# Keys of the latent attention formed channels first, with the weight columns stationary, in a two-block fp32 kernel on one core

## The chip, the core and the metric

The kernel runs on one core of one Trainium2 chip. The metric is the device time of one execution, in microseconds (us); the median of three executions of the kernel before is 2329.42 us (2329.14 to 2329.72). The core has TensorE (matrix products, PE in the profile, with PEld for its weight loads), VectorE (DVE), ScalarE (ACT), GpSimd (POOL) and SyncE (SP), which issues the DMAs. A matmul has a stationary operand, which a weight load puts into the array, and a moving operand, of which one column after another streams past it.

## The reference, cut to what matters

256 tokens of width 2048 go through a first block (pooling mixer, gated linear attention, a feed-forward part) and then through two layers of a second block. Only the second block's layers are touched by the change, and of them only the keys and values:

```python
for l in range(2):
    z = rmsnorm(x, pre_norm_g[l]) @ w_in[l]
    q_lat, kv_lat, k_pe, gb, gc, xin, q_mem, gate = split_cols(z)
    q = (rmsnorm(q_lat, q_norm_g[l]) @ w_uq[l]).reshape(b, s, 8, 192)
    kv = (rmsnorm(kv_lat, kv_norm_g[l]) @ w_ukv[l]).reshape(b, s, 8, 128 + 128)
    k_nope, v = kv[..., :128], kv[..., 128:]
    k = concatenate([k_nope, broadcast(apply_rope(k_pe, cos, sin))], axis=-1)
    a_out = mla_attention(q, k, v)      # softmax(q k^T / sqrt(192)) v, 8 heads
    ...
    x = x + rmsnorm(concatenate([a_out, c_out, m_out]) * silu(gate) @ w_o[l], post_norm_g[l])
```

`kv_lat` has 256 channels and `w_ukv` is 256 x 2048: for each of the 8 heads 128 columns of keys and 128 of values. The scores need the keys with the channels on the partitions; the product with the probabilities needs the values with the tokens on the partitions.

## The kernel before, in words

All products are made in fp32 precision from two fp32r parts each: a value is split into a high part and the rest (low), and a product is the sum of three matmuls, high by high, high by low and low by high. The weights are streamed from HBM once. `weight_groups` (from L92) lists them in the order of use as groups, mostly of 512 columns by 16 slices of 128 rows. A group's slices are its **steps**: `Plan` (from L180) numbers them through the whole kernel, and two steps of a group share a slab, one load into a buffer `raw`. ScalarE copies a slab to its high part `wh` (L1493), VectorE subtracts to get the low part `wl` (L2123), and TensorE uses both.

TensorE's main loop (in `tensor_program`, from L612) makes for each step the products for both halves of the 256 tokens: the activation slice (128 channels by 128 tokens) is stationary, the 512 weight columns move, and the output has the tokens on the partitions (L998 to L1000). That is six matmuls a step. The sums of a group lie in `pm`, two pairs of PSUM banks used in turn, so a group's sums must be taken out by the time the next group but one begins.

All else is **background work**, written by hand as generators with the step at which each piece is due: `layer(l)` exists once in each of `tensor_program`, `scalar_program` and `vector_program`. Each `yield L + n` means "when step n of this layer is reached", L being the first step of the group `ql`. TensorE does a piece in between its steps. ScalarE and VectorE do theirs ahead of the split of the slab that lies three slabs in front of that step (`Plan.ahead`, L208), and each engine's queue is strictly in order, so that a wait in a piece holds up the slabs behind it.

The steps of a layer are: ql 0 to 15 (query latents), kv 16 to 31 (key latents and rotary key), qm 32 to 47, a gate group 48 to 63, uq0 64 to 67, a gate group, uq1 84 to 87, **ukv0 88 and 89**, a gate group, uq2, **ukv1 110 and 111**, a gate group, uq3, **ukv2 132 and 133**, gc, **ukv3 150 and 151**, xi, gb, then the output product. `uq` j and `ukv` j hold the queries and the keys and values of two heads. `ROUNDS` (L245) has the steps of the six attention rounds: scores, turn of the probabilities, product with the values, turn of the output; rounds 2 to 5 use ukv0 to ukv3, and their scores are due at steps 96, 118, 140 and 158.

What happens to the keys before, for each of the four `ukv` groups of each of the two layers:

- The latents (group kv) are taken out of PSUM by ScalarE, scaled by the root of the earlier norm, their squares are summed (L1038), and VectorE (L1532) and GpSimd (`inverse_root`, L577) make the latents' own root from it, `rs["kv"]`. Meanwhile TensorE turns the unscaled latents at step 35 (`lat_turns`), ScalarE and VectorE make the high and low part of the turned latents with the norm's gain (`high_gain` and `low_gain`), `kvT`. At step 38 the rotary key is turned (`kp_t`).
- The main loop makes two steps of six matmuls of 512 columns with `kvT` stationary.
- `ukv_taken` (L1112): ScalarE takes the result, tokens first, in four instructions, scaling each token's row by `rs["kv"]`: keys to `S2` (L1126), values to `vt` (L1128).
- `uk_turn` (L861), at steps 93, 115, 137 and 155 (`UK`): TensorE turns the keys of two heads, four transposes of 128 by 128 (all transposes have the line of the helper `turn`, L628), into bank 7.
- `uk_copy` (L1131): ScalarE copies bank 7 to the high part of `kT` (L1136), VectorE subtracts for the low part (L1513, in `low`).
- The scores (L814 to L818) use `kT` as moving operand of 256 columns.

Of the kernel before, what the change touches and what calls it, by code (L numbers as in the profile page):

```python
# [14 lines left out]
T = 256  # L15
# [76 lines left out]
def weight_groups(a):  # L92
# [3 lines left out]
    def add(name, act, w, c0, n=512, kts=k16, **more):  # L96
        out.append(Group(name, act, [(w[:, c0:c0 + n], n)], kts, **more))
# [41 lines left out]
    for l in range(2):  # L139
# [7 lines left out]
        def ukv(j):  # L147
            add(f"ukv{l}{j}", "kvT", w_kv, 512 * j, kts=range(2), ev=("a", 4))

# [69 lines left out]
def counted(parts):  # L219

    out, n = {}, 0
    for name, w in parts:
# [23 lines left out]
          (158, 162, 165, 169))  # L246
UQ_N, UQ_R, UK = (71, 91, 113, 135), (79, 95, 117, 139), (93, 115, 137, 155)
S2_OF = {"ql": 0, "kv": 1, "qm": 0, "uq0": 1, "uq1": 0, "ukv0": 1, "uq2": 0, "ukv1": 1, "uq3": 0, "ukv2": 1, "gc": 0,
         "ukv3": 1}
SEMAPHORES = """mm hi lo ev_a ev_d nh sq st_r st_v rstd scl sq0 warm xsq xrd xss msq mrd mss hT_h hT_l pool_m wp_h wp_l dT_h dT paT_h paT_l gu g_h la_m la_d la_a qk_t  # L250
qk_c sc_m g_c sd sc_e e_m lev_m dg v_h at_d a_h av_m on_d oT_t oT_h oT_l sig mix_d mix_t mix_h mix_l mem_h mem_l rp rp_a xr xt_t
xt_h xt_l mk_t mk_c f_t f_h f_l fs_d sc mx ex rl pt_t pt_c pv ys yt_t y_h y_l ql_t ql_h ql_l kv_t kv_h kv_l kp_t kp_c qm_t
qm_c qm_l mk_h mk_l kp_l uq_t uq_c uq_l uqr_t uqr_c uqr_l uk_t uk_c uk_l u_t u_c cv_d gb_t gbm c_h c_l half d_id d_t0 d_t1 d_t2 d_t3 d_t4 d_t5 d_t6 d_gain d_pm d_wp d_wgu d_bg
d_cm d_bi0 d_bi1 d_bc d_pos d_m0 d_m1 d_m2 d_m3 d_x d_out""".split() + [f"raw{i}" for i in range(NRAW)]
# [357 lines left out]
def tensor_program(nc, s, m, p):  # L612
# [6 lines left out]
    def free(b):  # L619
        if b in bank:  # L620
            w.wait_ge(s[bank[b][0]], bank[b][1])
# [153 lines left out]
    def lat_turns(l, name, n, at0):  # L775

        S = m.S2[S2_OF[name]]
        for i in range(n):
            yield at0 + i
            free(6 + i)  # L780
            w.wait_ge(s["ev_a"], p.evac[f"{name}{l}"])
            turn_pair(6 + i, S, 2 * i).then_inc(s[f"{name}_t"], 1)
            bank[6 + i] = (f"{name}_l", (l * n + i + 1) * 2)

    def attention(l, r, which):

        idx = 2 * (6 * l + r)
        if which == 0:
# [15 lines left out]
            else:  # L804
                w.wait_ge(s["uq_l"], 4 * l + r - 1)
                w.wait_ge(s["uqr_l"], 2 * (4 * l + r - 1))
                w.wait_ge(s["uk_l"], 4 * l + r - 1)
                w.wait_ge(s["kp_l"], l + 1)
                w.wait_ge(s["ev_a"], p.evac[f"ukv{l}{r - 2}"])
                (qh_, ql_), (kh_, kl_) = m.qT[j], m.kT[j]  # L810
# [49 lines left out]

    def uk_turn(l, j):  # L861
        free(7)
        w.wait_ge(s["ev_a"], p.evac[f"ukv{l}{j}"])
        turn_pair(7, m.S2[S2_OF[f"ukv{j}"]], 0).then_inc(s["uk_t"], 1)
        bank[7] = ("uk_l", 4 * l + j + 1)

    def layer(l):
        L = p.first[f"ql{l}"]
        yield from lat_turns(l, "ql", 2, L + 19)
        yield from lat_turns(l, "kv", 1, L + 35)  # L870
        yield L + 38
        free(7)
# [20 lines left out]
        uq_turn(l, 1)  # L893
        yield L + UK[0]
        uk_turn(l, 0)
        yield L + UQ_R[1]
        uqr_turn(l, 1)
        for r in range(2, 6):
            for which in range(4):
                yield L + ROUNDS[r][which]  # L900
                attention(l, r, which)
            if r < 4:
                yield L + UQ_N[r]
                uq_turn(l, r)
            if r < 5:
                yield L + UK[r - 1]
                uk_turn(l, r - 1)
            if r < 4:
                yield L + UQ_R[r]
                uqr_turn(l, r)  # L910
# [40 lines left out]
    for i, g in enumerate(p.groups):  # L951
# [4 lines left out]
        for k in g.kts:  # L956
# [31 lines left out]
            elif n == 0:  # L988
                for x, y, sem in ((ah, h, "hi"), (al, h, "hT_l"), (ah, l, "lo")):
                    w.wait_ge(s[sem], 1)  # L990
                    for half in range(2):
                        ins = e.matmul(acc[:, half, :], x[:, 0, half * 128:half * 128 + 128], y[:, c], start=(sem == "hi"),
                                       stop=False)
            else:
                for half in range(1 if g.name == LAST else 2):
# [23 lines left out]
def scalar_program(nc, s, m, xT, lead, p):  # L1019
# [92 lines left out]
    def ukv_taken(l, j):  # L1112
        name = f"ukv{l}{j}"
        acc = m.pm[p.groups.index(p.g[name]) % 2]
        S = m.S2[S2_OF[f"ukv{j}"]]
        w.wait_ge(s["rstd"], RS[f"kv{l}"])
        w.wait_ge(s["mm"], p.end[name])
        if j == 0:
            w.wait_ge(s["sc"], 12 * l + 4)
            w.wait_ge(s["uq_t"], 4 * l + 1)  # L1120
            w.wait_ge(s["rp"], RP[f"uq{l}0"])
        else:
            w.wait_ge(s["uk_t"], 4 * l + j)
        for half in range(2):
            av = acc[:, half, :].rearrange("p (h d) -> p h d", h=2)
            e.activation(S[:, half, 0:256].rearrange("p (h d) -> p h d", h=2), av[:, :, 0:128], ACT.Copy,  # L1126
                         scale=m.rs[f"kv{l}"][:, half:half + 1]).then_inc(s["ev_a"], 1)
            e.activation(m.vt[:, half, 2 * j:2 * j + 2, :], av[:, :, 128:256], ACT.Copy,  # L1128
                         scale=m.rs[f"kv{l}"][:, half:half + 1]).then_inc(s["ev_a"], 1)

    def uk_copy(l, j):  # L1131
        w.wait_ge(s["uk_t"], 4 * l + j + 1)
        w.wait_ge(s["pv"], 12 * l + 4)
        if j >= 2:
            w.wait_ge(s["sc"], 12 * l + 2 * j + 2)
        e.activation(m.kT[j % 2][0][:, :, :], view(7), ACT.Copy).then_inc(s["uk_c"], 1)  # L1136

# [30 lines left out]
    def layer(l):  # L1168
# [19 lines left out]
        if l:  # L1188
            w.wait_ge(s["u_t"], 2)
            w.wait_ge(s["uk_t"], 4)  # L1190
        taken(0, f"ql{l}", m.S2[0], scale=f"r{r}")
# [9 lines left out]
        for half in range(2):  # L1201
            w.wait_ge(s["ev_a"], p.evac[f"kv{l}"])
            squares(m.S2[1][:, half, 0:256], m.ssq[f"kv{l}"][:, half:half + 1])
        yield L + 36
        w.wait_ge(s["kv_t"], l + 1)
        high_gain(6, m.kvT[0], 0, f"kv{l}", 0, "kv_h")
        w.wait_ge(s["mk_c"], 2 * l + 2)
        e.activation(m.mkS[0][:, :, :], m.mkT[l][:, :, :], ACT.Copy).then_inc(s["mk_h"], 1)
        yield L + 39
        w.wait_ge(s["kp_t"], l + 1)  # L1210
# [33 lines left out]
        uq_copy(l, 1)  # L1244
        yield L + UK[0] + 1
        uk_copy(l, 0)
        yield L + UQ_R[1] + 1
        uqr_copy(l, 1)
        for rr in range(2, 6):
# [18 lines left out]
            if rr < 4:  # L1268
                yield L + UQ_N[rr] + 1
                uq_copy(l, rr)  # L1270
            if rr < 5:
                yield L + UK[rr - 1] + 1
                uk_copy(l, rr - 1)
            if rr < 4:
# [227 lines left out]
def vector_program(nc, s, m, p):  # L1502
# [113 lines left out]
    def memory_low(n, c):  # L1616
        yield p.first[MEM_FROM[n]] + MEM_SPLITS[n][c] + 1
        piece = (m.memA, m.memB)[n][c // 2]
        if n:
            w.wait_ge(s["u_t"], 2)  # L1620
            w.wait_ge(s["uk_t"], 4)
            w.wait_ge(s["c_h"], 2)
            w.wait_ge(s["c_l"], 2)
# [113 lines left out]
    def layer(l):  # L1737
# [11 lines left out]
        if l:  # L1749
# [3 lines left out]
        e.tensor_copy(m.kpd[:, :, 64:128], m.kpd[:, :, 0:64]).then_inc(s["rp"], 1)  # L1753
        yield L + 36
        low_gain(6, m.kvT, 0, f"kv{l}", 0, "kv_h", 2 * l + 2, "kv_l")
        w.wait_ge(s["mk_h"], l + 1)
        e.tensor_tensor(m.mkS[1][:, :, :], m.mkT[l][:, :, :], m.mkS[0][:, :, :].bitcast(F32), ALU.subtract
                        ).then_inc(s["mk_l"], 1)
        yield L + 39
        low(7, m.kpeT, 0, 1, "kp_c", l + 1, "kp_l")  # L1760
# [3 lines left out]
        for r in range(6):  # L1764
# [33 lines left out]
            if 1 <= r <= 4:  # L1798
                yield L + UK[r - 1] + 1
                low(7, m.kT[(r - 1) % 2], 0, 2, "uk_c", 4 * l + r, "uk_l")  # L1800
            if 1 <= r <= 3:
# [394 lines left out]
```

## Time and profile before

| | us |
|---|---|
| median of three executions | 2329.42 (2329.14 to 2329.72) |
| the profiled execution's own time | 2329.7 |
| its span, first to last instruction | 2327.9 |
| around the span | 1.8 |
| TensorE busy | 2318.0 |
| TensorE weight loads busy | 1940.5 |
| VectorE busy | 1359.2 |
| ScalarE busy | 1180.9 |
| DMA engines' mean busy share | 62% |
| granted TensorE clock, mean | 0.999 of full |

A row of the timeline has the start of an instruction (or of a run of like ones, with their count) in us from the span's start, its duration in us, the engine, the line, what it writes and reads, the size of the stationary operand, and the partitions by columns of the moving one. Matmuls overlap: the end of one is modelled and lies behind the start of the next, so what a matmul costs in a dense stream is the distance from its start to the next one's start, not its duration.

### The profile page before, as it was taken

Reading aid. Unit: us, or ns where it says so; the run is one execution under the profiler, and the core shown is the slowest. Engines: PE = TensorE matmul, PEld = TensorE weight load, DVE = VectorE, ACT = ScalarE, POOL = GpSimd, SP = SyncE. Lnnn points to the kernel's source line nnn. Section 1 sums busy time; section 2 is a strip of 40 time slices with the busy share of each in tenths; the row PEclk is TensorE's granted clock in tenths of the full one; section 3 lists DMA queues with packets and bytes.
Section 4 is the critical chain, followed back from the end, with each engine's and each line's share of the span. In section 5 each row is a group of like instructions: output and inputs, shape, how many; then the busy total and the mean of one; then the engine's idle time right before and its main releaser. Section 6 shows DMA issues by size and latency. Waiting matters only on the chain.

```text
span 2327.9 us, 27235 instructions
## 1 busy us (share of the span) xinstructions
PE 2318.0 (100%) x10941; PEld 1940.5 (83%) x10941; DVE 1359.2 (58%) x1721; ACT 1180.9 (51%) x1565; POOL 25.6 (1%) x35
## 2 busy tenths in 40 slices
PE   9999999999999999999999999999999999999998
PEld 7888888888888888888888888888888888888887
DVE  6677666555566644554445555575555656565564
ACT  6555655444445744444444344465555456565543
POOL 0000000000000000000000000000000000000000
PEclk9999999999999999999999999999999999999999
DMA  8666665666667566665666666666555665655564
GB/s 292 189 176 172 173 171 176 195 200 199 191 206 268 173 192 190 190 189 190 192 190 192 191 190 206 223 179 191 158 159 163 199 217 154 196 162 150 157 204 136
DMA packets 237837, 438.87 MB, mean 189 GB/s; under 512 B 16688, under 2 KB 42800, under 8 KB 237072
## 3 DMA queue, kind: packets, MB, share of 16 engines
q1 hardware_dynamic: 237280, 436.61, 61.9%
q8 instruction: 86, 1.41, 0.2%
q10 hardware_dynamic: 432, 0.53, 0.1%
q14 instruction: 39, 0.32, 0.0%
HBM read 434.99 MB, written 2.10 MB: 188 GB/s over the span
## 4 chain that ended last, share of the span: by engine, by line
PE 99%; DMA 0%; DVE 0%; ACT 0%; SPq 0%; DVEq 0%; issue 0%; ACTq 0%
PE pm L998 31%; PE pm L1000 31%; PE pm L999 31%; PE pb L628 3%; PE pb L835 1%; PE pb L721 1%; PE pb L731 0%; DMA raw<-in_w_in 0%; PE pb L817 0%; PE pb L815 0%; PE pb L816 0%; PE pb L818 0%; PE pb L814 0%; PE pm L1015 0%; PE pm L1014 0%; PE pm L1016 0%
## 5 line engine op out<-in xcount | busy, mean ns | idle before, releaser
L2123 DVE TENSOR_TENSOR wl<-raw,wh 128x1024 fp32r<-128x1024 f32 (+3 forms) x786 | 949.2, 1211 | 846.2 <-ACT wh L1493 844.2
L1493 ACT ACTIVATE wh<-raw 128x1024 fp32r<-128x1024 f32 (+3 forms) x786 | 820.4, 1046 | 934.7 <-PE pm L1000 930.4
L998 PE MATMUL pm<-wh,hTh 128*128 128x512 f32 x702 | 277.4, 395 | 1.4 <-DVE wl L2123 1.3
L998 PE MATMUL pm<-wh,x2Th 128*128 128x512 f32 x704 | 275.3, 391 | 0.0
L1000 PE MATMUL pm<-wh,x2Tl 128*128 128x512 f32 x704 | 274.1, 389 | 0.0
L999 PE MATMUL pm<-wl,x2Th 128*128 128x512 f32 x704 | 274.0, 389 | 0.0
L1000 PE MATMUL pm<-wh,hTl 128*128 128x512 f32 x702 | 273.7, 390 | 0.0
L999 PE MATMUL pm<-wl,hTh 128*128 128x512 f32 x702 | 273.4, 389 | 0.0
L998 PE MATMUL pm<-wh,xT3h 128*128 128x512 f32 (+1 forms) x640 | 251.6, 393 | 0.0
L1000 PE MATMUL pm<-wh,xT3l 128*128 128x512 f32 (+1 forms) x640 | 245.0, 383 | 0.0
L999 PE MATMUL pm<-wl,xT3h 128*128 128x512 f32 (+1 forms) x640 | 244.5, 382 | 0.0
L998 PEld LDWEIGHTS pm<-wh,hTh 128*128 128x128 f32 x702 | 131.9, 188 | 29.2 <-DVE wl L2123 3.3
L1000 PEld LDWEIGHTS pm<-wh,x2Tl 128*128 128x128 f32 x704 | 132.2, 188 | 27.6
L1000 PEld LDWEIGHTS pm<-wh,hTl 128*128 128x128 f32 x702 | 131.8, 188 | 28.0
L999 PEld LDWEIGHTS pm<-wl,x2Th 128*128 128x128 f32 x704 | 132.2, 188 | 27.0
L998 PEld LDWEIGHTS pm<-wh,x2Th 128*128 128x128 f32 x704 | 132.2, 188 | 26.9
L999 PEld LDWEIGHTS pm<-wl,hTh 128*128 128x128 f32 x702 | 132.0, 188 | 25.8
L1000 PEld LDWEIGHTS pm<-wh,xT3l 128*128 128x128 f32 x640 | 120.1, 188 | 23.5
L999 PEld LDWEIGHTS pm<-wl,xT3h 128*128 128x128 f32 x640 | 120.6, 188 | 19.9
L998 PEld LDWEIGHTS pm<-wh,xT3h 128*128 128x128 f32 x640 | 120.4, 188 | 19.7
L998 PE MATMUL pm<-wh,yTh 128*128 128x512 f32 x240 | 93.7, 391 | 0.0
L1000 PE MATMUL pm<-wh,yTl 128*128 128x512 f32 x240 | 93.4, 389 | 0.0
(414 smaller groups left out, 3125.0 us busy)
## 6 DMA issues: line engine op xcount, KB each, us to landing
raw<-in_w_in SPq DMA_DIRECT2D x286, 512.0 KB, 3.7
raw<-in_w_ffn_gate SPq DMA_DIRECT2D x88, 512.0 KB, 4.3
raw<-in_w_ffn_up SPq DMA_DIRECT2D x88, 512.0 KB, 3.8
raw<-in_w_ffn_down SPq DMA_DIRECT2D x88, 512.0 KB, 4.1
raw<-in_w_o SPq DMA_DIRECT2D x64, 512.0 KB, 4.4
raw<-in_w_in SPq DMA_DIRECT2D x68, 256.0 KB, 3.2
raw<-in_w_branch_b SPq DMA_DIRECT2D x32, 512.0 KB, 3.7
raw<-in_w_out SPq DMA_DIRECT2D x32, 512.0 KB, 4.5
```

Source lines behind the costliest of these rows:

```text
L628: ins = e.transpose(pb[b][:, o:o + 128], src[half], ident[:, :])
L721: ins = e.matmul(pb[4 + i][:, j * 128:j * 128 + 128], E[:, 4 * i + j, 0, ft, :], E[:, 4 * i + j, 1, ft, :], start=(ft == 0), stop=(ft == 1))
L835: ins = e.matmul(pb[4 + ln][:, qh * 128:qh * 128 + 128], m.PT[ln][:, kk, qh * 128:qh * 128 + 128], v, start=(kk == 0), stop=(kk == 1))
L998: e.matmul(o, ah[:, kk, t], h[:, c], start=first, stop=False)
L999: e.matmul(o, ah[:, kk, t], l[:, c], start=False, stop=False)
L1000: ins = e.matmul(o, al[:, kk, t], h[:, c], start=False, stop=last)
L1493: e.activation(h[:, 0:n], r[:, 0:n], ACT.Copy).then_inc(s["hi"], 1)
L2123: e.tensor_tensor(l[:, 0:n], r[:, 0:n], h[:, 0:n].bitcast(F32), ALU.subtract).then_inc(s["lo"], 1)
```

## The change

The keys of the two heads of a `ukv` group are formed channels first, so that they need no turn. The columns of `w_ukv` are put in another order in HBM: in each group of 512 the keys of both heads come first, the values of both heads behind them. For the key columns the weight slice (128 rows by 128 columns) is now the stationary operand and the 256 tokens of `kvT` move; for the value columns the activation stays stationary and 256 weight columns move. A token's scale can no longer be applied per partition to keys whose tokens lie along the free dimension, so the latents themselves are scaled by `rs["kv"]` before they are turned. `uk_turn`, `uk_copy` and the staging of the keys in `S2` are gone; the latents' turn and what follows from it is due four steps later, the rotary key's three.

```diff
         def ukv(j):
-            add(f"ukv{l}{j}", "kvT", w_kv, 512 * j, kts=range(2), ev=("a", 4))
+            add(f"ukv{l}{j}", "kvT", w_kv, 512 * j, kts=range(2), ev=("d", 1))
...
-UQ_N, UQ_R, UK = (71, 91, 113, 135), (79, 95, 117, 139), (93, 115, 137, 155)
+UQ_N, UQ_R = (71, 91, 113, 135), (79, 95, 117, 139)
...   tensor_program, lat_turns
             w.wait_ge(s["ev_a"], p.evac[f"{name}{l}"])
+            if name == "kv":
+                w.wait_ge(s["kv_s"], 2 * l + 2)
...   tensor_program, attention (scores)
-                w.wait_ge(s["uk_l"], 4 * l + r - 1)
                 w.wait_ge(s["kp_l"], l + 1)
-                w.wait_ge(s["ev_a"], p.evac[f"ukv{l}{r - 2}"])
+                w.wait_ge(s["ev_d"], p.evac[f"ukv{l}{r - 2}"])
...
-    def uk_turn(l, j):
-        free(7)
-        w.wait_ge(s["ev_a"], p.evac[f"ukv{l}{j}"])
-        turn_pair(7, m.S2[S2_OF[f"ukv{j}"]], 0).then_inc(s["uk_t"], 1)
-        bank[7] = ("uk_l", 4 * l + j + 1)
...   tensor_program, layer (and its four calls of uk_turn are gone)
-        yield from lat_turns(l, "kv", 1, L + 35)
-        yield L + 38
+        yield from lat_turns(l, "kv", 1, L + 39)
+        yield L + 41
...   tensor_program, main loop
+            elif g.name.startswith("ukv"):
+
+                for b in range(2):
+                    o, c = acc[:, 0, b * T:(b + 1) * T], slice(at0 + b * 128, at0 + b * 128 + 128)
+                    e.matmul(o, h[:, c], ah[:, kk, :], start=first and b == 0, stop=False, skip_group_check=True)
+                    e.matmul(o, l[:, c], ah[:, kk, :], start=False, stop=False, skip_group_check=True)
+                    e.matmul(o, h[:, c], al[:, kk, :], start=False, stop=last, skip_group_check=True)
+                c = slice(at0 + 256, at0 + 512)
+                for half in range(2):
+                    o, t = acc[:, 1, half * T:(half + 1) * T], slice(half * 128, half * 128 + 128)
+                    e.matmul(o, ah[:, kk, t], h[:, c], start=first and half == 0, stop=False, skip_group_check=True)
+                    e.matmul(o, ah[:, kk, t], l[:, c], start=False, stop=False, skip_group_check=True)
+                    ins = e.matmul(o, al[:, kk, t], h[:, c], start=False, stop=last, skip_group_check=True)
...   scalar_program, ukv_taken
-        S = m.S2[S2_OF[f"ukv{j}"]]
-        w.wait_ge(s["rstd"], RS[f"kv{l}"])
         w.wait_ge(s["mm"], p.end[name])
-        if j == 0:
-            w.wait_ge(s["sc"], 12 * l + 4)
-            w.wait_ge(s["uq_t"], 4 * l + 1)
-            w.wait_ge(s["rp"], RP[f"uq{l}0"])
-        else:
-            w.wait_ge(s["uk_t"], 4 * l + j)
-        for half in range(2):
-            av = acc[:, half, :].rearrange("p (h d) -> p h d", h=2)
-            e.activation(S[:, half, 0:256].rearrange("p (h d) -> p h d", h=2), av[:, :, 0:128], ACT.Copy,
-                         scale=m.rs[f"kv{l}"][:, half:half + 1]).then_inc(s["ev_a"], 1)
-            e.activation(m.vt[:, half, 2 * j:2 * j + 2, :], av[:, :, 128:256], ACT.Copy,
-                         scale=m.rs[f"kv{l}"][:, half:half + 1]).then_inc(s["ev_a"], 1)
-
-    def uk_copy(l, j):
-        w.wait_ge(s["uk_t"], 4 * l + j + 1)
+        w.wait_ge(s["sc"], 12 * l + 4)
         w.wait_ge(s["pv"], 12 * l + 4)
         if j >= 2:
             w.wait_ge(s["sc"], 12 * l + 2 * j + 2)
-        e.activation(m.kT[j % 2][0][:, :, :], view(7), ACT.Copy).then_inc(s["uk_c"], 1)
+        e.activation(m.vt[:, :, 2 * j:2 * j + 2, :], acc[:, 1, :].rearrange("p (a h d) -> p a h d", a=2, h=2), ACT.Copy
+                     ).then_inc(s["uk_c"], 1)
+        e.activation(m.kT[j % 2][0][:, :, :], acc[:, 0, :].rearrange("p (n t) -> p n t", n=2), ACT.Copy
+                     ).then_inc(s["uk_c"], 1)
...   scalar_program, layer (and its calls of uk_copy are gone)
-        yield L + 36
+        yield L + 37
+        w.wait_ge(s["rstd"], RS[f"kv{l}"])
+        for half in range(2):
+            e.activation(m.S2[1][:, half, 0:256], m.S2[1][:, half, 0:256], ACT.Copy, scale=m.rs[f"kv{l}"][:, half:half + 1]
+                         ).then_inc(s["kv_s"], 1)
+        yield L + 40
         w.wait_ge(s["kv_t"], l + 1)
         high_gain(6, m.kvT[0], 0, f"kv{l}", 0, "kv_h")
         w.wait_ge(s["mk_c"], 2 * l + 2)
         e.activation(m.mkS[0][:, :, :], m.mkT[l][:, :, :], ACT.Copy).then_inc(s["mk_h"], 1)
-        yield L + 39
+        yield L + 42
         w.wait_ge(s["kp_t"], l + 1)
...   vector_program, layer (the latents' low part is due at L + 40 in place of 36, the rotary key's at 42 in place of 39)
             if 1 <= r <= 4:
-                yield L + UK[r - 1] + 1
-                low(7, m.kT[(r - 1) % 2], 0, 2, "uk_c", 4 * l + r, "uk_l")
+                yield p.end[f"ukv{l}{r - 1}"] + 1
+                w.wait_ge(s["uk_c"], 2 * (4 * l + r))
+                k, acc = m.kT[(r - 1) % 2], banks(f"ukv{l}{r - 1}")
+                e.tensor_tensor(k[1][:, :, :], acc[:, 0, :].rearrange("p (n t) -> p n t", n=2), k[0][:, :, :].bitcast(F32),
+                                ALU.subtract).then_inc(s["ev_d"], 1)
...   kernel (host side, order of the weight's columns)
+    arrays["w_ukv_2"] = np.ascontiguousarray(
+        arrays["w_ukv_2"].reshape(2, 256, 4, 2, 2, 128).transpose(0, 1, 2, 4, 3, 5)).reshape(2, 256, 2048)
```

Three waits on the removed semaphore `uk_t`, which guard the reuse of `S2` and of the memory pieces, become waits on `uq_t`.

## Rows read from the trace of the kernel before

**Rows 1.** The page: busy times, granted clock by slice, and the chain that ended last.

```profile
PE 2318.0 (100%) x10941; PEld 1940.5 (83%) x10941; DVE 1359.2 (58%) x1721; ACT 1180.9 (51%) x1565; POOL 25.6 (1%) x35
...
PEclk9999999999999999999999999999999999999999
...
PE 99%; DMA 0%; DVE 0%; ACT 0%; SPq 0%; DVEq 0%; issue 0%; ACTq 0%
```

**Rows 2.** All waits of TensorE in the whole span: us in total, times, longest.

```profile
PE pb L947 <- POOL warm L570: 1.3, 1, 1.3
PE pm L998 <- DVE wl L2123: 1.3, 2, 0.7
```

**Rows 3.** Timeline of TensorE, group ukv0 of the first layer, first and last of 12.

```profile
1684.48 0.39 PE L998 MATMUL pm<-wh,kvTh 128*128 128x512 f32 x1
...
1687.01 0.39 PE L1000 MATMUL pm<-wh,kvTl 128*128 128x512 f32 x1
1687.24 0.39 PE L998 MATMUL pm<-wh,xT3h 128*128 128x512 f32 x1
```

**Rows 4.** Timeline of TensorE, a turn of keys and the 18 matmuls behind it.

```profile
1793.63 0.60 PE L628 MATMUL pb<-ident,s 128*128 128x128 f32 x4
1793.98 0.48 PE L998 MATMUL pm<-wh,xT3h 128*128 128x512 f32 x1
1794.29 0.40 PE L999 MATMUL pm<-wl,xT3h 128*128 128x512 f32 x1
...
1797.97 0.39 PE L1000 MATMUL pm<-wh,xT3l 128*128 128x512 f32 x1
1798.19 0.28 PE L814 MATMUL pb<-kT1h,qT1h 128*128 128x256 f32 x1
```

**Rows 5.** Timeline of TensorE, 18 matmuls of 512 columns, nothing between; first and last.

```profile
1700.39 0.39 PE L998 MATMUL pm<-wh,xT3h 128*128 128x512 f32 x1
...
1704.25 0.39 PE L1000 MATMUL pm<-wh,xT3l 128*128 128x512 f32 x1
```

**Rows 6.** Timeline of TensorE, 20 score matmuls: the first, and the matmul behind them.

```profile
1696.61 0.28 PE L814 MATMUL pb<-kT0h,qT0h 128*128 128x256 f32 x1
...
1699.01 0.40 PE L998 MATMUL pm<-wh,xT3h 128*128 128x512 f32 x1
```

**Rows 7.** The same for the 48 matmuls of the low-rank gate group, weights stationary.

```profile
57.11 0.28 PE L985 MATMUL pm<-hTh,wh 128*96 128x256 f32 x1
...
62.76 0.40 PE L998 MATMUL pm<-wh,hTh 128*128 128x512 f32 x1
```

**Rows 8.** Weight loads of one score line: ns min/median/max, first and last start.

```profile
L815 PEld LDWEIGHTS pb<-kT0l,qT0h x16: 188/188/192, 1696.6 to 2161.9; 128*128 128x128 f32 x16
```

**Rows 9.** The keys' and values' way through ScalarE and VectorE, by tile, same columns.

```profile
L1126 ACT ACTIVATE s<-pm,st x16: 473/475/476, 1687.5 to 2182.9; 128x256 f32<-128x256 f32 x16
L1128 ACT ACTIVATE vt<-pm,st x16: 467/475/482, 1687.9 to 2183.3; 128x256 f32<-128x256 f32 x16
L1136 ACT ACTIVATE kT0h<-pb x4: 598/598/600, 1692.4 to 2155.9; 128x512 fp32r<-128x512 f32 x4
L1513 DVE TENSOR_TENSOR kT0l<-pb,kT0h x4: 691/692/692, 1693.1 to 2156.5; 128x512 fp32r<-128x512 f32 x4
```

**Rows 10.** Timelines of ScalarE, GpSimd, VectorE and TensorE around the latents' turn.

```profile
1600.76 0.42 ACT L1038 ACTIVATE junk<-s 128x256 f32<-128x256 f32 x1
...
1601.17 2.00 ACT L1493 ACTIVATE wh<-raw 128x1024 fp32r<-128x1024 f32 x2
1603.78 0.84 ACT L1047 ACTIVATE kvTh<-pb,gain 128x256 fp32r<-128x256 f32 x2 [0.61 <-PE pb L628]
...
1601.55 0.77 POOL L577 TENSOR_TENSOR st<-st 128x2 f32<-128x2 f32 x1 [13.43 <-DVE st L1532]
...
1606.74 1.22 DVE L2123 TENSOR_TENSOR wl<-raw,wh 128x1024 fp32r<-128x1024 f32 x1
...
1613.39 0.39 PE L998 MATMUL pm<-wh,xT3h 128*128 128x512 f32 x1
```

More of the change, by code:

```diff
@@ L246 @@
           (158, 162, 165, 169))
-UQ_N, UQ_R, UK = (71, 91, 113, 135), (79, 95, 117, 139), (93, 115, 137, 155)
-S2_OF = {"ql": 0, "kv": 1, "qm": 0, "uq0": 1, "uq1": 0, "ukv0": 1, "uq2": 0, "ukv1": 1, "uq3": 0, "ukv2": 1, "gc": 0,
-         "ukv3": 1}
+UQ_N, UQ_R = (71, 91, 113, 135), (79, 95, 117, 139)
+S2_OF = {"ql": 0, "kv": 1, "qm": 0, "uq0": 1, "uq1": 0, "uq2": 0, "uq3": 0, "gc": 0}
 SEMAPHORES = """mm hi lo ev_a ev_d nh sq st_r st_v rstd scl sq0 warm xsq xrd xss msq mrd mss hT_h hT_l pool_m wp_h wp_l dT_h dT paT_h paT_l gu g_h la_m la_d la_a qk_t
@@ L252 @@
 xt_h xt_l mk_t mk_c f_t f_h f_l fs_d sc mx ex rl pt_t pt_c pv ys yt_t y_h y_l ql_t ql_h ql_l kv_t kv_h kv_l kp_t kp_c qm_t
-qm_c qm_l mk_h mk_l kp_l uq_t uq_c uq_l uqr_t uqr_c uqr_l uk_t uk_c uk_l u_t u_c cv_d gb_t gbm c_h c_l half d_id d_t0 d_t1 d_t2 d_t3 d_t4 d_t5 d_t6 d_gain d_pm d_wp d_wgu d_bg
+qm_c qm_l mk_h mk_l kp_l uq_t uq_c uq_l uqr_t uqr_c uqr_l kv_s uk_c u_t u_c cv_d gb_t gbm c_h c_l half d_id d_t0 d_t1 d_t2 d_t3 d_t4 d_t5 d_t6 d_gain d_pm d_wp d_wgu d_bg
 d_cm d_bi0 d_bi1 d_bc d_pos d_m0 d_m1 d_m2 d_m3 d_x d_out""".split() + [f"raw{i}" for i in range(NRAW)]
@@ L893, in layer @@
         uq_turn(l, 1)
-        yield L + UK[0]
-        uk_turn(l, 0)
         yield L + UQ_R[1]
@@ L904, in layer @@
                 uq_turn(l, r)
-            if r < 5:
-                yield L + UK[r - 1]
-                uk_turn(l, r - 1)
             if r < 4:
@@ L1189, in layer @@
             w.wait_ge(s["u_t"], 2)
-            w.wait_ge(s["uk_t"], 4)
+            w.wait_ge(s["uq_t"], 4)
         taken(0, f"ql{l}", m.S2[0], scale=f"r{r}")
@@ L1244, in layer @@
         uq_copy(l, 1)
-        yield L + UK[0] + 1
-        uk_copy(l, 0)
         yield L + UQ_R[1] + 1
@@ L1270, in layer @@
                 uq_copy(l, rr)
-            if rr < 5:
-                yield L + UK[rr - 1] + 1
-                uk_copy(l, rr - 1)
             if rr < 4:
@@ L1620, in memory_low @@
             w.wait_ge(s["u_t"], 2)
-            w.wait_ge(s["uk_t"], 4)
+            w.wait_ge(s["uq_t"], 4)
             w.wait_ge(s["c_h"], 2)
@@ L1753, in layer @@
         e.tensor_copy(m.kpd[:, :, 64:128], m.kpd[:, :, 0:64]).then_inc(s["rp"], 1)
-        yield L + 36
+        yield L + 40
         low_gain(6, m.kvT, 0, f"kv{l}", 0, "kv_h", 2 * l + 2, "kv_l")
@@ L1758, in layer @@
                         ).then_inc(s["mk_l"], 1)
-        yield L + 39
+        yield L + 42
         low(7, m.kpeT, 0, 1, "kp_c", l + 1, "kp_l")
```

## The prediction

> **What bounds the kernel.** I read the page first. TensorE is busy for 2318.0 of 2327.9 us, the chain that ended last is 99% TensorE, and the granted clock stands at its full level in all slices [rows 1]. Busy time of matmuls can hide gaps, since their ends are modelled, so the second view is that of the waits: TensorE waits twice, 1.3 us each, both in the lead-in or the first block, and never in the two layers that the change touches [rows 2]. So the time of these layers is the sum of the distances between the starts of TensorE's instructions. What ScalarE, VectorE or GpSimd gain or lose costs nothing until it makes TensorE wait. The third view, the timeline of TensorE, gives the prices of the instructions that are swapped.
>
> **Prices on TensorE.** All are start-to-start distances.
> - A matmul of 512 columns in an undisturbed stream: 1704.25 - 1700.39 = 3.86 us for 17 distances, 0.227 us each [rows 5].
> - A `ukv` group before, 12 matmuls of 512 columns: 1687.24 - 1684.48 = 2.76 us, 0.230 each [rows 3].
> - A turn of keys, four transposes: from its start to the first score matmul are 1798.19 - 1793.63 = 4.56 us, and the 18 matmuls of 512 columns in between would take 18 x 0.2271 = 4.09 without it [rows 4, 5]. So a turn costs 0.47 us: 0.35 to the next matmul's start, 0.31 - 0.23 = 0.08 more on that one, and a remainder in the next few.
> - A matmul of 256 columns with 128 stationary columns: (1699.01 - 1696.61) / 20 = 0.120 us [rows 6]. With weights stationary (96 columns) and the activations moving, the very form that the keys take: (62.76 - 57.11) / 48 = 0.118 us [rows 7].
>
> **The sum, part by part.** There are 4 groups in each of 2 layers, 8 in all.
> 1. Removed: 8 turns of keys, 8 x 0.47 = 3.8 us. Nothing covers them, since they stand in TensorE's own stream. Their steps (93, 115, 137, 155) lie two steps or more from any other turn, so each one has its own tail to lose.
> 2. Changed: each group's 12 matmuls of 512 columns become 24 of 256. The columns that stream are the same, but the part of a matmul that doesn't scale with columns is paid twice as often. 24 x 0.120 = 2.88 us in place of 2.76, so +0.12; I add 0.02 for the first long matmul behind short ones (the one behind the scores starts within a dense run as well, so this is an estimate from the 0.23 against 0.227 of rows 3 and 5). +0.14 a group, 8 x 0.14 = +1.1 us. I take 0.120 and not 0.118, as the stationary operand is 128 columns wide again. The bounds: 24 x 0.118 = 2.83 (+0.07 a group, +0.6 in all) below, and above, half of a matmul of this group and the whole fixed part worked out below on top, 0.230 / 2 + 0.013 = 0.128 [rows 3], should the switch between two kinds of stationary operand or two PSUM banks cost something: 3.07, +0.31 a group, +2.5 in all.
> 3. Moved: the turn of the latents from step 35 to 39 and that of the rotary key from 38 to 41. The same instructions at another place in the same dense stream: 0. They still have slack, for `kvT` is first read at step 88 and the rotary key at 96. The copies of `mkS` move with them and are first read at step 56. No DMA moves; the reordered weight has the same loads.
> 4. Added on ScalarE: two scalings of the latents, about 0.42 us each by the squares of the same size [rows 10], and a wait for the latents' root. In ScalarE's queue the piece due at step 37 stands before the same slab as the piece at 36 did, where the kernel before waited for the turn until 1603.78 and idled 0.61 us. The root leaves GpSimd at 1601.55 + 0.77 = 1602.32, before ScalarE has even finished the two splits that start at 1601.17 and end at 1603.17 [rows 10]. So the new wait is met about 0.8 us before it is asked. Behind it in the queue stands the split of the slab for steps 42 and 43; its low part was finished at 1606.74 + 1.22 = 1607.96 and TensorE first uses it at 1613.39, a lead of 5.4 us [rows 10]. The scalings take the place of the copy that has moved away. Cost 0; if the cover were gone, only what exceeds 5.4 us would reach TensorE.
> 5. Removed from ScalarE: four takings of 0.475 us per group become one of 512 elements, about 0.60 by the copy of the same size; the copy to `kT` and VectorE's subtraction stay at 0.60 and 0.69 [rows 9], but read the group's own sums. ScalarE gains about 1.3 us a group, 10 us in all, and it isn't the bound: 0. The keys are ready earlier: before, they left for a turn at 93, with copy and subtraction behind it; now both follow the group's end at 90. The last group's (152) stand against scores due at 158, six steps of 1.36 us.
> 6. The sums' banks are now freed by VectorE's subtraction (`ev_d`), one step behind the group. The next user is the next group but one, 16 steps or more later: 0.
>
> Sum: -3.8 + 1.1 = -2.7 us. The profiled execution took 2329.7 us (span 2327.9 and 1.8 around it) and goes to 2327.0; against the median of 2329.42, which lies 0.3 below it, that is 2326.7.
>
> **A rule against the trace.** Rows 5 and 6 show a fixed part: 0.227 us for 512 columns and 0.120 for 256 leave 0.227 - 2 x (0.227 - 0.120) = 0.013 us per matmul that doesn't scale with the columns. The Trainium skill, "TensorE: Matmul & The Clock Gate", section "Back-to-back issue gap", has N/2.4 + 2.5 ns for a warm matmul, so a fixed part five times smaller. By that page, halving the columns and doubling the count would cost 12 x 2.5 ns = 0.03 us a group and 0.24 in all, and the sum would be about -3.5; the trace contradicts the figure, and the sum above goes by the trace.
>
> **Rivals.**
> - *The whole gain shows, or more* (faster by over 0.2%, that is over 4.7 us; about what a measurement of this kernel can tell from no change). Turns at 3.8, the lower bound of part 2 (+0.6), and a loss of the 0.003 us by which the matmuls near the keys' turns and in the groups are slower than undisturbed ones [rows 3, 5] for some 20 matmuls around each of 8 groups (0.5): -3.7. It takes a further 1 us from something the rows don't show. 2325.7 as worked out, 2324.5 if over the bound. Chance of passing 0.2%: 0.06.
> - *The freed time comes back as waits*, so that nothing is gained: TensorE reaches its steps sooner and finds a slab not yet split. For it: VectorE and ScalarE are busy over half of the span [rows 1]. Against it: no wait in these layers now, and a lead of 5.4 us at a crowded place [rows 2, 10], against 0.5 us gained at a time. 2329.4. Chance 0.05.
> - *The short matmuls are bound by their weight loads* (slower). A load takes 0.188 us [rows 8], longer than the 0.120 between two short matmuls. Were the loads not overlapped where the stationary operand comes from `wh` and `wl`, which ScalarE and VectorE are writing to at the same time in other slots, a group would take 24 x 0.188 = 4.51 us, 1.75 more than before, 8 x 1.75 = +14.0, less 3.8 for the turns: +10.2, 2339.6. It turns into a loss from (2.76 + 0.47) / 24 = 0.135 us per matmul on, and into one of over 0.2% from (2.76 + 0.47 + 4.7 / 8) / 24 = 0.159. Against it: the scores have the same loads and hold 0.120 for 20 in a row, and the gate group has the weights stationary at 0.118 [rows 6, 7]. Chance 0.04.
> - *The turns aren't really saved*, since the change only moves work: excluded by the diff; four transposes a group are gone and none is added.
>
> **How the numbers follow.** The forecast, -2.7 us, is 0.12% and lies within 0.2%; its chance, with its bounds, is 0.85. Its own range: best, -3.8 + 0.6 less 0.5 for the slower neighbours = -3.7; worst, with 0.128 per short matmul and turns at 0.43 (0.35 + 0.08 without the remainder), -3.4 + 2.5 = -0.9. From 2329.42 that is 2325.7 to 2328.5; the runs scatter by 0.3 either way. To hold the time 8 times in 10 I take 2325.3 to 2328.7, which leaves out the slow rival, the case without any gain and the part of the fast one beyond its terms. Faster by over 0.2%: 0.06. Slower by over 0.2%: 0.04. Within 0.2%: 0.90.
>
> **What the new profile would show.** Right: 32 transposes fewer (10941 matmuls become 10941 - 32 + 96 = 11005, apart from records missing); a `ukv` group of 24 rows that takes 2.85 to 2.95 us from its first start to the next group's; no wait of TensorE in the two layers; undisturbed matmuls at 0.227 still; ScalarE busy about 10 us less. Part 4 is wrong if ScalarE idles before the scaling for the root, or TensorE waits for `wl` or `kvT` around steps 37 to 45. Part 2 is wrong if the short matmuls stand more than 0.128 apart, and then the loads' start times say whether the load is late. The forecast as a whole fails if TensorE waits anywhere for more than a microsecond in the layers, or if the clock falls below its full level.

## The result and the profile after

The changed kernel takes 2326.31 us (median of 22 executions, 2326.05 to 2326.66) against 2329.80 us (22 executions, 2329.14 to 2330.28) of the kernel before on the same chips: 3.5 us less, a ratio of 0.9985 (95% interval 0.9979 to 0.9992). The forecast was 2326.7, no change beyond 0.2%, and the measured change is 0.15%. It was worked out as 2.7 us less than 2329.42; the 22 executions put the kernel before 0.4 us above that base, so the forecast time is closer (0.4 us) than the forecast difference (0.8 us). The profiled execution took 2326.3 us with a span of 2324.5 us.

The page of the changed kernel, the lines that answer to [rows 1], and all waits of TensorE, which answer to [rows 2]:

```profile
PE 2314.6 (100%) x11005; PEld 1943.7 (84%) x11005; DVE 1358.8 (58%) x1721; ACT 1174.0 (51%) x1545; POOL 25.5 (1%) x35
...
PEclk9999999999999999999999999999999999999999
...
PE 99%; DMA 0%; DVE 0%; ACT 0%; SPq 0%; issue 0%; DVEq 0%; ACTq 0%
```

```profile
PE pm L1000 <- DVE wl L2115: 1.4, 3, 0.8
PE pb L936 <- POOL warm L569: 1.3, 1, 1.3
```

The 11005 matmuls are the 10941 - 32 + 96 of the prediction. TensorE is still the whole chain, at the full clock, and its few waits lie ahead of the two layers: cut to the layers, the list of waits is empty for this kernel and for every experiment below, though the last experiment has a short wait that this list doesn't show. ScalarE is 6.9 us less busy.

The timeline of TensorE around ukv0 of the first layer, which answers to [rows 3]: the 24 matmuls of 256 columns, the 6 long ones behind them, the turn of a pair of queries, and the place where the turn of the keys stood.

```profile
1684.08 0.28 PE L987 MATMUL pm<-kvTh,wh 128*128 128x256 f32 x1
1684.20 0.28 PE L988 MATMUL pm<-kvTh,wl 128*128 128x256 f32 x1
1684.32 0.28 PE L989 MATMUL pm<-kvTl,wh 128*128 128x256 f32 x1
...
1684.79 0.28 PE L993 MATMUL pm<-wh,kvTh 128*128 128x256 f32 x1
...
1686.95 0.40 PE L1000 MATMUL pm<-wh,xT3h 128*128 128x512 f32 x1
...
1688.34 0.60 PE L627 MATMUL pb<-ident,s 128*128 128x128 f32 x4
1688.69 0.48 PE L1000 MATMUL pm<-wh,xT3h 128*128 128x512 f32 x1
...
1694.26 0.38 PE L627 MATMUL pb<-ident,rope_o 128*128 128x128 f32 x2
...
1695.86 0.28 PE L814 MATMUL pb<-kT0h,qT0h 128*128 128x256 f32 x1
```

The group takes 1686.95 - 1684.08 = 2.87 us, 0.120 per matmul, whether the weights (L987 to L989) or the activations (L993 to L995) are stationary. Before it took 2.76 [rows 3]. The six long matmuls behind it take 1688.34 - 1686.95 = 1.39, where the kernel before has 1.36:

```profile
1687.24 0.39 PE L998 MATMUL pm<-wh,xT3h 128*128 128x512 f32 x1
...
1688.60 0.60 PE L628 MATMUL pb<-ident,s 128*128 128x128 f32 x4
1688.96 0.48 PE L998 MATMUL pm<-wh,xT3h 128*128 128x512 f32 x1
...
1691.80 0.60 PE L628 MATMUL pb<-ident,s 128*128 128x128 f32 x4
1692.15 0.48 PE L998 MATMUL pm<-wh,xT3h 128*128 128x512 f32 x1
...
1695.01 0.38 PE L628 MATMUL pb<-ident,rope_o 128*128 128x128 f32 x2
```

These are the rows of the kernel before at the same place; the second transpose row is the keys' turn. From the first long matmul behind the queries' turn to the rotary part's turn there are 24 long matmuls in both: 1695.01 - 1688.96 = 6.05 us before, 1694.26 - 1688.69 = 5.57 after. One turn of keys cost 0.48 us there.

ScalarE and GpSimd around the latents' scaling, which answer to [rows 10]:

```profile
1600.36 0.42 ACT L1040 ACTIVATE junk<-s 128x256 f32<-128x256 f32 x1
...
1600.78 1.99 ACT L1482 ACTIVATE wh<-raw 128x1024 fp32r<-128x1024 f32 x2
1604.36 1.06 ACT L1482 ACTIVATE wh<-raw 128x1024 fp32r<-128x1024 f32 x1 [1.60 <-PE pm L1002]
1605.33 0.89 ACT L1196 ACTIVATE s<-s,st 128x256 f32<-128x256 f32 x2
...
1608.82 0.84 ACT L1049 ACTIVATE kvTh<-pb,gain 128x256 fp32r<-128x256 f32 x2 [0.68 <-PE pb L627]
```

```profile
1601.15 0.77 POOL L576 TENSOR_TENSOR st<-st 128x2 f32<-128x2 f32 x1 [13.44 <-DVE st L1521]
```

The root is there at 1601.92 and the scaling begins at 1605.33, right behind a split and with no idle time before it. The wait is met 3.4 us early.

The values and keys are now taken by one instruction each, which answer to [rows 9]:

```profile
L1122 ACT ACTIVATE vt<-pm x8: 598/598/599, 1687.1 to 2179.4; 128x512 f32<-128x512 f32 x8
...
L1124 ACT ACTIVATE kT0h<-pm x4: 591/591/591, 1687.6 to 2148.9; 128x512 fp32r<-128x512 f32 x4
L1791 DVE TENSOR_TENSOR kT0l<-pm,kT0h x4: 679/680/682, 1691.0 to 2152.2; 128x512 fp32r<-128x512 f32 x4
```

### The profile page after: what moved, and what is told of

It is laid out like the page before. It is cut to its first block, busy times and chain, and to the rows that moved or that the text cites. A ratio compares the mean times of both kernels' runs of the same rounds, so it can differ in the third digit from the quotient of the medians.

```text
span 2324.5 us, 27335 instructions
## 1 busy us (share of the span) xinstructions
PE 2314.6 (100%) x11005; PEld 1943.7 (84%) x11005; DVE 1358.8 (58%) x1721; ACT 1174.0 (51%) x1545; POOL 25.5 (1%) x35
## 4 chain that ended last, share of the span: by engine, by line
PE 99%; DMA 0%; DVE 0%; ACT 0%; SPq 0%; issue 0%; DVEq 0%; ACTq 0%
PE pm L1000 30%; PE pm L1002 30%; PE pm L1001 30%; PE pb L627 3%; PE pb L835 1%; PE pb L720 1%; PE pb L730 0%; DMA raw<-in_w_in 0%; PE pb L817 0%; PE pb L815 0%; PE pm L989 0%; PE pm L994 0%; PE pm L995 0%; PE pm L993 0%; PE pb L816 0%; PE pm L988 0%
```

## A ruler for half a microsecond

Medians of this kernel scatter by a few tenths, as much as some of the effects. The traces give a finer ruler. The first turn of the query latents in the first layer of the second block (step 19, the first row below) and the last matmul of the program (the second row) are the same instructions in all versions, and all instructions that the change touches lie between them. The kernel before, in its first profiled execution:

```profile
1586.72 0.60 PE L628 MATMUL pb<-ident,s 128*128 128x128 f32 x4
...
2320.37 0.39 PE L1016 MATMUL pm<-wh,yTl 128*128 128x512 f32 x1
```

and the changed kernel:

```profile
1586.32 0.60 PE L627 MATMUL pb<-ident,s 128*128 128x128 f32 x4
...
2317.02 0.39 PE L1018 MATMUL pm<-wh,yTl 128*128 128x512 f32 x1
```

The stretch is 733.65 us before and 730.70 after: **2.95 us** are gained in it, and 0.40 us of the traces' difference already stand at its start, where the edit changes nothing. Each experiment below is read on this ruler too; the two profiles of each of these two kernels agree on it to 0.01 us.

## The experiments

**The two kernels once more.**

> The kernel before once more, as a yardstick for the lead-in and the first block, in which the changed kernel's trace is 0.40 us ahead although the edit touches nothing there. Theory A (that part of the trace differs from execution to execution): this trace's first block, against the other trace of the same kernel, is off by some tenths too, either way. Rival (the 0.40 belongs to the build, since another program is laid out otherwise): this trace agrees with the other of the same kernel within 0.1 us up to step ql of the first layer. Time 2329.4 to 2330.0 us by both.

> The changed kernel once more, as a yardstick for its own trace and for the next runs. Theory A: 2326.3 us within 0.3; the distance to the kernel before inside the two layers is 2.9 to 3.0 us as in the first pair of traces, and what lies ahead of them differs by some tenths from the other trace of the same kernel. Rival (the 0.40 us in the first block belongs to the build): the first block is again 0.4 us ahead of the kernel before.

Measured: 2329.85 us (11 executions) for the kernel before, 2326.35 us (11) for the changed one. The new profile of the kernel before:

```profile
1586.47 0.60 PE L628 MATMUL pb<-ident,s 128*128 128x128 f32 x4
...
2320.12 0.39 PE L1016 MATMUL pm<-wh,yTl 128*128 128x512 f32 x1
```

The stretch is again 733.65; that of the changed kernel's second profile is 2317.21 - 1586.51 = 730.70 again. What lies ahead of it moves by 0.25 us between two profiles of the kernel before (1586.72 and 1586.47) and by 0.19 between two of the changed one (1586.32 and 1586.51), so most of the 0.40 us of the first pair is scatter of the lead-in, as theory A had it. Not all of it lies in the first microseconds: from the first long matmul behind the low-rank gate group [rows 7] (62.76 and 62.62 us in the two profiles of the kernel before, 62.58 and 62.75 in those of the changed one) to the stretch's start are 1523.96 and 1523.85 us before, 1523.74 and 1523.76 after. Two profiles of one kernel differ by 0.11 us there, the two kernels by 0.1 to 0.2, and the builds of the experiments below have 1523.75 to 1524.09 at the same place. So builds and executions both move this part, by tenths of a microsecond, where no edit touches it.

**Only the latents' scaling and the moves.** The kernel before with part 3 and 4 of the prediction alone; the keys are still made tokens first and turned. The four takings of each `ukv` group no longer scale the tokens, and VectorE's low parts move with the turns (not in the cut of the edit).

```diff
-        yield from lat_turns(l, "kv", 1, L + 35)
-        yield L + 38
+        yield from lat_turns(l, "kv", 1, L + 39)      # waits for kv_s
+        yield L + 41
...
-        yield L + 36
+        yield L + 37
+        w.wait_ge(s["rstd"], RS[f"kv{l}"])
+        for half in range(2):
+            e.activation(m.S2[1][:, half, 0:256], m.S2[1][:, half, 0:256], ACT.Copy, scale=m.rs[f"kv{l}"][:, half:half + 1]
+                         ).then_inc(s["kv_s"], 1)
+        yield L + 40
```

> The kernel before with only the latents' scaling ahead of their turn, the turn moved from step 35 to 39 and the rotary key's from 38 to 41; keys still tokens first and turned. Theory A: nothing, 2329.8 within 0.2 us; ScalarE doesn't idle for the root. Rival (these moves give the part of the gain, some 0.4 us, that the turns and the split matmuls don't explain): 2329.4 or less, seen as a gain between steps 32 and 48 of each layer.

Measured: 2329.56 us against 2329.63 of the kernel before on this chip; stretch 2320.16 - 1586.51 = 733.65 us, the same as before. So the moves and the new wait are worth nothing, either way.

**Only the split of the matmuls.** The kernel before, with each 512-column matmul of the `ukv` groups in two halves.

```diff
+            elif g.name.startswith("ukv"):
+                for half in range(2):
+                    t = slice(half * 128, half * 128 + 128)
+                    for b in range(2):
+                        o, c = acc[:, half, b * T:(b + 1) * T], slice(at0 + b * T, at0 + (b + 1) * T)
+                        e.matmul(o, ah[:, kk, t], h[:, c], start=first and b == 0, stop=False, skip_group_check=True)
+                        e.matmul(o, ah[:, kk, t], l[:, c], start=False, stop=False, skip_group_check=True)
+                        ins = e.matmul(o, al[:, kk, t], h[:, c], start=False, stop=last, skip_group_check=True)
```

> The kernel before with each matmul of 512 columns of the ukv groups split into two of 256 with the same stationary activation; turns kept. Theory A (a fixed part of 0.013 us per matmul; measured +0.106 us a group in the changed kernel): 8 x 0.11 = +0.9 us on the kernel before, 2330.7. Rival 1 (the skill's figure of 2.5 ns): +0.24, 2330.0. Rival 2 (the extra belongs to weights as stationary operand, not to the count): +0.2 or less, 2330.0.

Measured: 2330.88 us, 1.25 above the kernel before (2329.63); the stretch has 2321.38 - 1586.66 = 734.72 us, +1.07. The group, and the first long matmul and the turn behind it:

```profile
1684.42 0.28 PE L999 MATMUL pm<-wh,kvTh 128*128 128x256 f32 x1
...
1687.29 0.40 PE L1006 MATMUL pm<-wh,xT3h 128*128 128x512 f32 x1
...
1688.68 0.60 PE L628 MATMUL pb<-ident,s 128*128 128x128 f32 x4
```

2.87 us for the group and 1.39 behind it, the very numbers of the changed kernel. So the price of the change, 1.07 us or 0.134 for each of 8 groups, is that of the count alone: 0.106 in the group (mean of the eight) and 0.028 behind it. Which operand is stationary plays no part, which rules out rival 2. By the figure of 2.5 ns that the prediction cites from the Trainium skill ("TensorE: Matmul & The Clock Gate", section "Back-to-back issue gap") it would have been a quarter of this.

**Only the turns put back.** The changed kernel with four transposes of the identity where each turn of keys stood.

```diff
+    def idle_turn():
+        free(7)
+        for j in range(2):
+            turn(7, j, [ident[:, :], ident[:, :]])
...
+        yield L + UK[0]
+        idle_turn()
```

> The changed kernel with four transposes of a constant put in at each of the eight places where the keys' turn stood (bank 7, no reader). Theory A: each costs 0.46 us as the trace of before says, so 8 x 0.46 = 3.7 us more than the changed kernel, 2330.0 us, which is 0.2 to 0.8 us above the kernel before (the price of the split matmuls, less what differs outside the layers). Rival (a turn costs only its own 0.35 us and the rest of the difference was waits): 8 x 0.35 = 2.8 more, 2329.1.

Measured: 2330.56 us, 4.2 above the changed kernel (2326.35); stretch 2321.51 - 1586.79 = 734.72 us, +4.02 on the changed kernel's 730.70, so 0.50 us per turn. At the place of [rows 4] this run has the turn and the scores behind its 18 long matmuls at

```profile
1794.23 0.60 PE L627 MATMUL pb<-ident 128*128 128x128 f32 x4
...
1798.80 0.28 PE L814 MATMUL pb<-kT1h,qT1h 128*128 128x256 f32 x1
```

and the changed kernel has the same 18 matmuls and the scores at

```profile
1792.31 0.39 PE L1000 MATMUL pm<-wh,xT3h 128*128 128x512 f32 x1
...
1796.39 0.28 PE L814 MATMUL pb<-kT1h,qT1h 128*128 128x256 f32 x1
```

4.57 us against 4.08: the turn costs 0.49 there. Taken from one round's first score to the next, the four turns of the first layer cost 0.49, 0.48, 0.48 and 0.49. Another 0.09 us build up in steps of 0.01 to 0.03 between the first layer's last scores and the second layer's first ones, near other turns, and 0.05 behind the last scores of the second layer. Why is open. The stretch of 734.72 is that of the split experiment to the hundredth, as it must be if the change is nothing but these two terms: -4.02 + 1.07 = -2.95.

**Each turn made twice**, in the kernel before:

```diff
-        turn_pair(7, m.S2[S2_OF[f"ukv{j}"]], 0).then_inc(s["uk_t"], 1)
+        for _ in range(2):
+            ins = turn_pair(7, m.S2[S2_OF[f"ukv{j}"]], 0)
+        ins.then_inc(s["uk_t"], 1)
```

> The kernel before with each turn of keys made twice in a row into the same bank. Theory A (a turn is four transposes of 0.088 us and a tail of about 0.11 on the long matmuls behind it, paid once per turn however long): 8 x 0.35 = +2.8 us on the kernel before, 2332.6. Rival (the tail belongs to each transpose): 8 x 0.46 = +3.7, 2333.5.

Measured: 2333.35 us, +3.6 on 2329.75; stretch 2323.39 - 1586.30 = 737.09, +3.44, which is 0.43 per second turn. The sum lies between the two, nearer the rival's, but the rival's reason isn't the one that the rows show. One such double turn:

```profile
1691.38 1.03 PE L628 MATMUL pb<-ident,s 128*128 128x128 f32 x8
1692.17 0.48 PE L1000 MATMUL pm<-wh,xT3h 128*128 128x512 f32 x1
...
1694.99 0.38 PE L628 MATMUL pb<-ident,rope_o 128*128 128x128 f32 x2
```

Eight transposes take 0.79 us to the next matmul's start, against 0.35 for four: the second four cost 0.44, or 0.11 each, not 0.088. The twelve long matmuls behind them take 2.82 us where those behind a single turn take 2.86 (1695.01 - 1692.15, above). Undisturbed, twelve would take 2.72, so the tail is 0.14 us behind four transposes and 0.10 behind eight. That can be read so: a transpose in a longer run costs 0.11 us, the first few are cheaper by a part of what the long ones behind them then pay, and the rest of the tail is paid once. No run takes these parts asunder.

**A long contraction.** The changed kernel with the memory queries (16 slices) made channels first too, without their two turns a layer; the tokens' scale of these queries is left out.

```diff
-        add(f"qm{l}", "xT3", w_i, 2368, ev=("a", 2))
+        add(f"qm{l}", "xT3", w_i, 2368, ev=("d", 2))
...
+            elif g.name.startswith("qm"):
+                for b in range(4):
+                    o, c = acc[:, b // 2, b % 2 * T:(b % 2 + 1) * T], slice(at0 + b * 128, at0 + b * 128 + 128)
+                    e.matmul(o, h[:, c], ah[:, kk, :], start=first and b % 2 == 0, stop=False, skip_group_check=True)
...
-            turn_pair(6 + i, m.S2[S2_OF["qm"]], 2 * i).then_inc(s["qm_t"], 1)
```

> The changed kernel with the memory attention's queries (group qm, 16 slices of 512 columns) formed channels first as well, without their two turns; the tokens' scale of these queries is left out. It tests whether the exchange pays for a long contraction. Theory A: a step's 6 matmuls of 512 columns become 12 of 256, 12 x 0.120 - 6 x 0.227 = +0.078 us at most and +0.053 by what the ukv groups showed, 16 steps: +0.85 to +1.25; two turns less, -0.92; so -0.1 to +0.3 a layer, -0.2 to +0.7 in all: 2326.1 to 2327.0, no gain. Rival 1 (the split costs little): 8 turns-pairs' price, -1.8, 2324.5. Rival 2 (long dense stretches of short matmuls are slower than 0.120 apart, as their weight loads never get ahead): a loss of several us.

Measured: 2326.87 us, 0.5 above the changed kernel; stretch 2317.63 - 1586.50 = 731.13, +0.43. So the exchange loses here, within the range that theory A gives for the sum of both terms. It is 0.22 us a layer; if the two turns are worth 0.50 each, the split cost (0.22 + 1.00) / 16 = 0.076 us a slice, an estimate that is above the 0.067 of the `ukv` groups. Short matmuls are no slower in a long run: the group has 192 of them from

```profile
1598.82 0.28 PE L980 MATMUL pm<-xT3h,wh 128*128 128x256 f32 x1
...
1622.50 0.40 PE L1000 MATMUL pm<-wh,xT3h 128*128 128x512 f32 x1
```

and with the turns that fall into it (the latents', four transposes, and the rotary key's, two) each slot is (1622.50 - 1598.82) / 198 = 0.120 us.

**A version meant to beat both.** Keys of four heads in one group, all short; values of four heads in another, all long.

```diff
         def ukv(j):
-            add(f"ukv{l}{j}", "kvT", w_kv, 512 * j, kts=range(2), ev=("d", 1))
+            add(f"uv{l}{j}", "kvT", w_kv, 1024 * j, kts=range(2), ev=("a", 2))
+            add(f"uk{l}{j}", "kvT", w_kv, 1024 * j + 512, kts=range(2), ev=("d", 2))
...
         ukv(0)
         gt(1)
         uq(2)
-        ukv(1)
         gt(2)
         uq(3)
-        ukv(2)
+        ukv(1)
         add(f"gc{l}", "xT3", w_i, 1344, ev=("a", 2))
-        ukv(3)
```

> A version meant to beat both: the keys of four heads form one group (24 matmuls of 256 columns a group, weights stationary), the values of four heads another (12 of 512 columns, activations stationary), two of each a layer, so that a layer has 48 short and 24 long matmuls in place of 96 short ones. Theory A (fixed part per matmul, about 0.0132 us): a layer's 24 long ones in place of 48 short save 24 x 0.0132 = 0.3 us, -0.6 us on the changed kernel, 2325.7. Rival 1 (fixed part 2.5 ns): -0.12, 2326.2. Rival 2 (slower): the value group's banks are needed again two steps after its end, 2.7 us, and ScalarE takes them in two instructions of 0.6 us; if it is late, TensorE waits at steps 92 and 136, up to 1 us at four places, 2327 to 2330.

Measured: 2326.38 us, the same as the changed kernel (2326.35); stretch 2317.12 - 1586.59 = 730.53 us, -0.17 in place of -0.6. The waits for the value group's banks that rival 2 names aren't there, but another one is (below). The value group takes 2.76 us as in the kernel before:

```profile
1684.35 0.39 PE L993 MATMUL pm<-wh,kvTh 128*128 128x512 f32 x1
...
1687.11 0.28 PE L986 MATMUL pm<-kvTh,wh 128*128 128x256 f32 x1
```

so the count does what it should there. A part of the loss is seen behind `uq2`, whose place the new order of groups has changed:

```profile
1722.24 0.39 PE L993 MATMUL pm<-wh,xT3h 128*128 128x512 f32 x1
...
1723.69 0.63 PE L626 MATMUL pb<-ident,s 128*128 128x128 f32 x4
1724.08 0.48 PE L993 MATMUL pm<-wh,xT3h 128*128 128x512 f32 x1
```

Six long matmuls take 1.45 us and the turn 0.39, where the changed kernel has 1.39 and 0.35 at ukv0: 0.1 us a layer. The other engines' rows show why. ScalarE takes `uq2`'s sums (first row), and the weight loads stand still before the one of the turn (second row):

```profile
1722.50 1.05 ACT L1049 ACTIVATE s<-pm,st 128x384 f32<-128x384 f32 x2 [0.54 <-PE pm L995]
...
1723.66 0.42 PEld L626 LDWEIGHTS pb<-ident,s 128*128 128x128 f32 x4 [0.31 <-issue]
```

In the changed kernel, whose turn starts at 1723.49, the same taking is

```profile
1719.49 1.05 ACT L1056 ACTIVATE s<-pm,st 128x384 f32<-128x384 f32 x2 [1.00 <-PE pm L1002]
```

In the new order one step and not three lies between the end of `uq2` and its turn. The taking ends at 1722.50 + 1.05 = 1723.55, and the load begins 0.11 us later; in the changed kernel the taking is done 3 us before the turn. By the code (`uq_turn` waits for the taking), this is a wait of TensorE for ScalarE. It comes once in each layer (the second at 2114.56), the loads of no other version have an idle stretch in the layers, and the list of waits misses it because the profile calls it "issue". The rest of the loss lies behind the last scores of each layer: there the version is 0.15 us ahead of the changed kernel in both layers, and 0.08 and 0.05 of it are gone by the end. Why that is so stays open. The version as it stands is a tie; the same groups with this turn a step or two later were not run.

## Why the prediction was right, point by point

- **What bounds it** (TensorE's own stream, no wait): right. The stretch that holds the change is reproduced to 0.01 us in the repeated profiles of both kernels, and in them and in the one-term experiments it moves only with TensorE's instructions.
- **Part 1, the turns** (-3.8, 0.47 each): right in kind, 6% too small. The runs show 0.50 each, -4.02. The step that was mis-sized is the tail. It isn't the choice of the place [rows 4]: the same turn, with and without, costs 0.49 there and 0.48 to 0.49 at the three other places of the layer. About 0.02 were lost because the 18 matmuls were priced at 0.2271 each (4.09), where without the turn they take 4.08 and with it 4.57 (4.56 in the rows used); the other 0.01 to 0.02 per turn show only far behind it, beyond the layer's last scores.
- **Part 2, the split** (+0.12 in the group and 0.02 behind it, +1.1): right; measured 0.106 and 0.028, +1.07. The choice of 0.120 over 0.118 for the weights-stationary form was right, and so was the fixed part read from rows against the Trainium skill's 2.5 ns: 12 extra matmuls cost 0.134 us, 0.011 each. The estimate of -3.5 us by that page of the Trainium skill happens to be the measured median difference, by luck: the two terms, each measured alone, are -4.02 and +1.07.
- **Part 3, the moves**: 0, shown by an experiment with nothing else.
- **Part 4, the wait for the root**: no cost, right, but the place in ScalarE's queue was one slab off: the piece due at step 37 comes behind the split that I had put after it, since step 36 and 37 share a slab and a piece is done once the step behind it is reached. The margin was 3.4 us and not 0.8.
- **Part 5**: no cost, right, but ScalarE's busy time fell by 6.9 us and not 10. Two things were missing. Instructions in a row overlap, so their durations don't add up: the four takings of a group start 0.36 us apart (1687.49, 1687.86, 1688.22, 1688.58, and the next instruction at 1688.93), 1.44 us in all and not 4 x 0.475, and with the copy of 0.60 that makes 2.04; the two instructions of the changed kernel take 0.97 (1687.15 to 1688.12). That is 8 x 1.07 = 8.6 us. The scalings that part 4 adds, 4 x 0.44 = 1.8, weren't taken off it, and 8.6 - 1.8 = 6.8.
- **The rivals**: the freed time did not come back as waits (no wait in the layers); the weight loads did not bind (24 short matmuls 0.120 apart). The fast rival's direction is in part what happened: the turns are worth 0.2 us more than 3.8.
- **What is not explained**: of the 3.5 us between the medians, 2.95 lie in the layers. The rest lies outside. It isn't the turns, the split or the moves. The median less the stretch is 1596.15 us for the kernel before and 1595.61 for the changed one (1596.20 and 1595.65 in their repetitions), and 1595.74 to 1596.26 for the builds of the experiments, so a part of it may go with the build; the lead-in scatters by 0.2 us or so as well. Nothing here parts the two. The 0.5 us were not forecast.

## What to carry to other kernels

In a kernel that TensorE bounds without a wait, a turn that feeds a product can be priced against the split that avoids it: here a turn of 256 by 256 costs 0.50 us, and splitting the 512 columns of one slice of the contraction costs 0.067 (0.134 for two slices) to 0.076 (estimated from the 16 slices). One turn against 2 slices pays; two turns against 16 slices lose (measured +0.43 us for two layers). Take the price of a burst of small matmuls from the same place with and without it, up to where the stream is back at its undisturbed pace, and expect a few hundredths more far behind it. When groups change places, look at how many steps lie between a group's end and the first background piece that reads it. For effects below the scatter of the medians, measure the stretch between two instructions that all versions share.

## What the runs showed of the hardware

- A matmul has a part that doesn't scale with its columns: two of 256 columns take 0.011 us more than one of 512 in the `ukv` groups (0.134 us for 12), whichever operand is stationary.
- Transposes of 128 by 128 in a row are not equally dear: four take 0.35 us to the next matmul, eight take 0.79 and, in a run, each further one 0.11. The Trainium skill, "TensorE: Matmul & The Clock Gate", section "LDWEIGHTS (loading the stationary operand)", gives columns / 1.2 ns for a load; worked out from it, an estimate, 128 columns take 107 ns. The distance of 0.11 us is close to it, but the loads' own rows last 0.188 us [rows 8] and 0.14 us for a transpose, and no run here changes the width of a load. So it isn't shown that the load sets the distance.
- The last 734 us are reproduced closely: the stretch is 733.65 us in both profiles of the kernel before and in that of the version with only the moves, and 730.70 in both of the changed kernel. The 1524 us ahead of it differ by 0.11 us between two profiles of one kernel.
